# Where the split weights and their activations start within 128 bytes of SBUF

## The chip, the cores and the metric

The kernel runs on one core of one Trainium2 chip. TensorE multiplies, VectorE and ScalarE split operands and do the pointwise work, GpSimd (POOL) issues the gathers, SyncE (SP) issues the weight transfers. The metric is the device time of one launch in microseconds, the median of three runs.

## The reference

One token block of 256 tokens x 2048 channels goes through two layers in float32. Everything below is computed by this kernel in one launch (cut to what matters):

```python
def first_block(x, ...):                      # gated linear attention, then SwiGLU
    h = rms_norm(x, g0)
    x = x + gla_mixer(h, w_in, ...) @ w_out   # w_in: 2048 x 6144 (+16)
    x = x + (silu(g) * u) @ w_down            # g, u = split(rms_norm(x, g1) @ w_gu), 2 x 5632 wide

def hybrid_layer(h, mem, ...):
    proj = rmsnorm(h, norm_mix) @ w_in        # queries, keys, values of two attentions
    o_nsa = nsa_attention(...)                # compressed, selected and window branches
    o_sb = stick_breaking_attention(q_sb, k_sb, v_sb)
    h = h + concatenate([o_nsa, o_sb]) @ w_out
    h = h + memory_attention(rmsnorm(h, g), rmsnorm(mem, g2), w_q, w_k, w_v, w_o)
    h = h + peer_ffn(rmsnorm(h, g3), w_pq, sub_keys, u_tab, v_tab)
    return h                                  # then one last rmsnorm

def peer_ffn(hn, w_pq, sub_keys, u_tab, v_tab):
    # 8 heads x 16 experts of 16384 per token: a row of u_tab for the hidden value,
    # a row of v_tab for the output
    a = einsum('td,ted->te', x, u_tab[expert])
    return einsum('te,ted->td', gate * gelu(a), v_tab[expert])
```

## The kernel before

**Tiles.** All dense weights come as one stream of 292 tiles of 1 MB ([128 partitions, 2048 numbers], that is 512 rows by 512 columns of a weight matrix, 4 row blocks of 128 by 512 columns). SyncE brings them into a ring of four slots, `ring`. ScalarE rounds each half tile (a unit) to the short float format of TensorE's fast mode and writes it to `WH` (L487 to L490, with the norm's gain as scale in most stages); VectorE writes what rounding left, weight minus leading part, to `WL` (L502, L506). Each of `WH` and `WL` holds four units of 4096 bytes per partition, two tiles in all.

**Activations** are split in the same way into a leading and a remaining part, turned so that channels lie on the partitions: `HH` and `HL`, [128, 16, 256] each, for all normed inputs and for the output of the stick-breaking attention, and pairs in the arena for others: `Y_h`/`Y_l` (output of the linear attention), `A_h`/`A_l` (the SwiGLU hidden values), `N_h`/`N_l` (output of the first attention), `MN_h`/`MN_l` (normed memory) and `MO_h`/`MO_l` (output of the memory attention).

**The product.** `three` (L608 in the profile) issues three matmuls for each pair: leading x leading, leading x rest, rest x leading. `chunk` has two forms. In form T the weights are stationary (128 x 128) and the activations move (256 columns): 4 row blocks x 4 column blocks x 3 = 48 matmuls a tile. In form N the activations are stationary (128 tokens) and the weights move (512 columns): 4 row blocks x 2 token blocks x 3 = 24 matmuls a tile. In the profile's names the moving operand comes first: `ps<-WH,HH` is form N, `ps<-HH,WH` form T.

| stage | us in the trace | tiles, form | activations |
|---|---|---|---|
| linear attention, input | 12 to 345 | 16 T, 32 N | HH, HL |
| linear attention, output | 346 to 445 | 16 N | Y |
| gate and up | 445 to 935 | 88 N | HH, HL |
| down | 935 to 1185 | 44 N | A |
| second block, input | 1196 to 1508 | 32 T, 12 N | HH, HL |
| attentions' output | 1509 to 1618 | 8 N, 8 N | N; HH, HL |
| memory keys, values, query | 1618 to 1695 | 4 T, 4 N, 4 T | MN, MN; HH, HL |
| memory output | 1706 to 1729 | 4 N | MO |
| expert query | 1731 to 1830 | 16 T | HH, HL |

(The four tiles of the compression weights are used unsplit, at L916.) After that the expert stage gathers rows of `peer_u` and `peer_v` by token into twelve slots of `rows`, which lie over ring, WH, WL, HL and HH. VectorE takes dot products (L2449) and scaled sums (L2453) of them, TensorE takes the rest of the sums and 32 dense rows as products in full float32 (L1241, L1230, L1221).

**Order.** Nothing is scheduled by a tool: each engine's program is written out by hand with its waits, and the order of all instructions is that of the source.

**Places.** `place` puts a tensor at a byte address of the partition, one after the other; `take` cuts pieces from `arena`, and `split_views` makes the arena's pairs. All pieces of the arena that concern this change are multiples of 128 bytes long, so they start where the arena starts within 128 bytes:

```python
        rows, _ = place("rows", [P, ROWS, D])
        ring, at = place("ring", [P, RING, TILE], at=at)
        WH, at = place("WH", [P, UNITS, UNIT], f32r, at)
        WL, at = place("WL", [P, UNITS, UNIT], f32r, at)
        HL, at = place("HL", [P, KD, TOK], f32r, at)
        HH, at = place("HH", [P, KD, TOK], f32r, at)
```

## Time and profile before

| | us |
|---|---|
| median of 3 runs | 3087.81 |
| lowest and highest run | 3081.02, 3088.20 |
| span of the profiled execution, first to last instruction | 3083.2 |
| TensorE busy in it | 2723.6 |
| VectorE busy in it | 2111.9 |

A profiled execution is one run with the profiler on; its span leaves out what lies before the first and after the last instruction. Matmuls overlap: one is on record for 280 to 400 ns, from its first read to its last write, while the next one starts long before that. How fast TensorE goes is therefore read from the distance between two starts, in the view of instructions in order of time, and not from the duration of one. Some matmul records are missing from the trace, so counts are taken from the program.

### The profile page before, as it was taken

Reading aid. Unit: us, or ns where it says so; the run is one execution under the profiler, and the core shown is the slowest. Engines: PE = TensorE matmul, PEld = TensorE weight load, DVE = VectorE, ACT = ScalarE, POOL = GpSimd, SP = SyncE. Lnnn points to the kernel's source line nnn. Section 1 sums busy time; section 2 is a strip of 40 time slices with the busy share of each in tenths; the row PEclk is TensorE's granted clock in tenths of the full one; section 3 lists DMA queues with packets and bytes.
Section 4 is the critical chain, followed back from the end, with each engine's and each line's share of the span. In section 5 each row is a group of like instructions: output and inputs, shape, how many; then the busy total and the mean of one; then the engine's idle time right before and its main releaser. Section 6 shows DMA issues by size and latency. Waiting matters only on the chain.

```text
span 3083.2 us, 34652 instructions
## 1 busy us (share of the span) xinstructions
PE 2723.6 (88%) x12212; PEld 1969.0 (64%) x12212; DVE 2111.9 (68%) x2870; ACT 1146.2 (37%) x1980; POOL 988.0 (32%) x567
## 2 busy tenths in 40 slices
PE   9999999999999999999999975666666877669997
PEld 8888788888887888999889872222223433235433
DVE  5687665555564545445566688887888887679877
ACT  5455555555553335445665530000002330034000
POOL 0021000000000000000000038777778777878864
PEclk9999999999999999999999997898999888988999
DMA  7444455555555555453354459999999999999997
GB/s 271 151 155 164 173 178 183 189 190 190 190 177 191 184 185 183 178 182 135 127 191 173 164 228 415 419 409 410 408 417 411 416 407 402 420 376 383 409 402 305
DMA packets 123586, 827.89 MB, mean 269 GB/s; under 512 B 22167, under 2 KB 22183, under 8 KB 23855
## 3 DMA queue, kind: packets, MB, share of 16 engines
q0 software_dynamic: 79392, 510.36, 40.8%
q1 hardware_dynamic: 43920, 313.73, 28.5%
q10 hardware_dynamic: 144, 2.10, 0.2%
q8 instruction: 78, 1.28, 0.2%
q14 instruction: 52, 0.43, 0.0%
HBM read 892.00 MB, written 4.22 MB: 291 GB/s over the span
## 4 chain that ended last, share of the span: by engine, by line
PE 58%; POOL 14%; DMA 11%; DVE 9%; issue 5%; ACT 3%; DVEq 0%; SPq 0%; ACTq 0%
PE ps L608 49%; POOL rows L1324 14%; DMA rows<-peer_u,arena 7%; PE ps L1230 2%; DMA rows<-peer_v,arena 2%; DMA rows<-peer_v 2%; DVE arena L2449 2%; PE ps L1241 2%; DVE WL L506 1%; PE ps L716 1%; ACT arena L1800 1%; DVE arena L209 1%; DVE arena L202 1%; PE ps L916 0%; DVE arena L203 0%
## 5 line engine op out<-in xcount | busy, mean ns | idle before, releaser
L506 DVE SCALAR_TENSOR_TENSOR WL<-ring,PA,WH 128x512 fp32r<-128x512 f32 x896 | 633.1, 753 | 461.7 <-ACT WH L490 445.1
L1241 PE MATMUL ps<-rows,rstd 128*128 128x512 f32 x1164 | 629.6, 694 | 300.1 <-DMA rows<-peer_v,arena 216.9
L2449 DVE CUSTOM_DVE_ANT_0 arena<-rows,arena 128x2048 f32<-128x2048 f32 x256 | 586.9, 2293 | 155.7 <-DMA rows<-peer_u,arena 128.9
L1241 PEld LDWEIGHTS ps<-rows,rstd 128*128 128x128 f32 x1164 | 245.8, 221 | 670.5 <-issue 371.9
L1324 POOL DMA_INDIRECT rows<-peer_v,arena x256 | 484.0, 1891 | 196.8 <-DVE arena L2449 73.4
L489 ACT ACTIVATE WH<-ring,PA 128x512 fp32r<-128x512 f32 x448 | 324.2, 724 | 550.1 <-PE ps L608 401.7
L1324 POOL DMA_INDIRECT rows<-peer_u,arena x256 | 451.4, 1763 | 165.7 <-DVE WL L506 85.9
L608 PE MATMUL ps<-WH,HH 128*128 128x512 f32 x1120 | 442.8, 395 | 4.0 <-DVE WL L506 4.0
L608 PE MATMUL ps<-WH,HL 128*128 128x512 f32 x1120 | 438.0, 391 | 0.0
L608 PE MATMUL ps<-WL,HH 128*128 128x512 f32 x1120 | 437.9, 391 | 0.0
L490 ACT ACTIVATE WH<-ring,PA 128x512 fp32r<-128x512 f32 x448 | 317.2, 708 | 0.0
L608 PE MATMUL ps<-HH,WH 128*128 128x256 f32 x1088 | 310.2, 285 | 6.3 <-DVE WL L506 4.7
L608 PE MATMUL ps<-HH,WL 128*128 128x256 f32 x1088 | 308.6, 284 | 0.0
L608 PE MATMUL ps<-HL,WH 128*128 128x256 f32 x1088 | 308.5, 284 | 0.0
L2453 DVE SCALAR_TENSOR_TENSOR XR<-rows,arena,XR 128x2048 f32<-128x2048 f32 (+1 forms) x112 | 260.2, 2324 | 52.4 <-DMA rows<-peer_v,arena 42.6
L1297 POOL DMA_DIRECT2D arena<-bias_rows x2 | 1.8, 908 | 905.5 <-DVE XR L2157 905.5
L502 DVE TENSOR_TENSOR WL<-ring,WH 128x1024 fp32r<-128x1024 f32 x128 | 155.9, 1224 | 166.0 <-ACT WH L487 165.4
L1789 ACT ACTIVATE rstd<-CO,arena 128x128 f32<-128x128 f32 x147 | 53.6, 396 | 551.2 <-PE ps L1241 533.9
L608 PEld LDWEIGHTS ps<-WH,HH 128*128 128x128 f32 x1120 | 211.4, 189 | 49.2 <-DVE WL L506 5.4
L608 PEld LDWEIGHTS ps<-WH,HL 128*128 128x128 f32 x1120 | 211.4, 189 | 44.6
L608 PEld LDWEIGHTS ps<-WL,HH 128*128 128x128 f32 x1120 | 211.5, 189 | 43.2 <-issue 0.5
L1230 PE MATMUL ps<-rows,arena 128*128 128x512 f32 x512 | 223.8, 597 | 10.1 <-DMA rows<-peer_v 10.0
(367 smaller groups left out, 3538.0 us busy)
## 6 DMA issues: line engine op xcount, KB each, us to landing
ring<-stream SPq DMA_DIRECT2D x292, 1024.0 KB, 4.8
rows<-peer_v POOLq DMA_DIRECT2D x32, 1024.0 KB, 15.4
rows<-peer_u,arena POOLq DMA_INDIRECT x256, 14.8
rows<-peer_v,arena POOLq DMA_INDIRECT x256, 15.0
arena<-xT SPq DMA_DIRECT2D x4, 512.0 KB, 9.3
bias_rows<-bias_scratch POOLq DMA_DIRECT2D x1, 2048.0 KB, 10.5
arena<-xT ACTq DMA_DIRECT2D x1, 2048.0 KB, 9.5
arena<-memT POOLq DMA_DIRECT2D x1, 2048.0 KB, 10.7
```

The costliest lines, as they stand in the source:

```text
L202: ch.post(V.max_index(i[:, 0:8], v[:, 0:8], s))
L489: nc.scalar.activation(half_tile(WH, u)[:, 0:CH], raw_half(u)[:, 0:CH], ACT.Copy, scale=gain[0])
L490: nc.scalar.activation(half_tile(WH, u)[:, CH:UNIT], raw_half(u)[:, CH:UNIT], ACT.Copy, scale=gain[1]).then_inc(hi_done, 1)
L502: nc.vector.tensor_tensor(half_tile(WL, u), raw_half(u), half_tile(WH, u).bitcast(f32), ALU.subtract).then_inc(split, 1)
L506: ins = nc.vector.scalar_tensor_tensor(out=half_tile(WL, u)[:, s], in0=raw_half(u)[:, s], scalar=gain[d], in1=half_tile(WH, u).bitcast(f32 ...
L608: last = mm(o, l, r, start=start and n == 0, stop=stop and n == 2)
L1230: last = mm(ps[:, 4 * tt + q, :], DENSE_H[tt][:, c, :], rows[:, SLOTS[n % ROWS], q * CH:(q + 1) * CH], start=tt == 0 and c == 0, stop=tt = ...
L1241: last = mm(ps[:, 4 * tt + q, :], DIAG[:, k % DIAGS, :], rows[:, SLOTS[n % ROWS], q * CH:(q + 1) * CH], start=n == mine[0], stop=n == ends[q])
L1324: nc.gpsimd.indirect_dma_start(out=rows[:, SLOTS[n % ROWS], :], out_offset=None, in_=u_tab if tab == "u" else v_tab, in_offset=bass.Indire ...
L1789: A(DIAG[:, k % DIAGS, :], ident, ACT.Copy, scale=GA[:, g // PEER_H, at:at + 1]).then_inc(sem("diagonals"), 1)
L2449: ins = V.tensor_tensor_reduce(out=JUNK, in0=rows[:, SLOTS[n % ROWS], :], in1=HN[:, tt, :], scale=1.0, scalar=0.0, op0=ALU.mult, op1=ALU.a ...
L2453: ins = V.scalar_tensor_tensor(out=XN[:, tt, s], in0=rows[:, SLOTS[n % ROWS], s], scalar=GA[:, tt, at:at + 1], in1=XN[:, tt, s], op0=ALU.m ...
```

## The change

It changes addresses and nothing else: every engine's list of instructions, waits and DMAs is the same row by row; only the tensors that they name have other places.

| bytes past a multiple of 128 | before | after |
|---|---|---|
| WH, WL | 0 | 32 |
| HH, HL, linear attention input | 0 | 32 |
| HH, HL, gate and up (norm1) | 0 | 0 |
| HH, HL, second block input (norm2) | 0 | 64 |
| HH, HL, stick-breaking output (sb) | 0 | 0 |
| HH, HL, memory query and expert query (norm3, norm4) | 0 | 64 |
| arena, and Y, A, N, MO in it | 32 | 0 |
| MN | 32 | 32 |
| slots of ring and rows | 0 | 0, 64 by turns |
| rstd | 32 | 32 |
| XR | 0 | 0 |

HH and HL become six pairs of views, one for each use, over the same space (`H_AT`). The slots of `ring` and `rows` grow from 8192 to 8256 bytes (`SLOT`), so that the space of two slots holds WH, WL, HL or HH with up to 128 bytes to spare (`PAIR`). What that takes from the arena is won back: `GE` and `DGM` move to the place of small weights whose time does not overlap theirs, `CA` and `EQ` of the expert choice to `rstd`.

```diff
+SLOT = TILE + 16
+PAIR = 2 * 4 * SLOT
+W_SHIFT = 32
...
-        rows, _ = place("rows", [P, ROWS, D])
-        ring, at = place("ring", [P, RING, TILE], at=at)
-
-
-        WH, at = place("WH", [P, UNITS, UNIT], f32r, at)
-        WL, at = place("WL", [P, UNITS, UNIT], f32r, at)
-        HL, at = place("HL", [P, KD, TOK], f32r, at)
-        HH, at = place("HH", [P, KD, TOK], f32r, at)
-        XR, at = place("XR", [P, TT, D], at=at)
+        rows_all, end = place("rows", [P, ROWS, SLOT])
+        rows = rows_all[:, :, 0:D]
+        ring_all, at = place("ring", [P, RING, SLOT], at=at)
+        ring = ring_all[:, :, 0:TILE]
+
+
+        WH, _ = place("WH", [P, UNITS, UNIT], f32r, at + W_SHIFT)
+        WL, _ = place("WL", [P, UNITS, UNIT], f32r, at + PAIR + W_SHIFT)
+        H_AT = {}
+        for name, shift in (("gla", 32), ("norm1", 0), ("norm2", 64), ("sb", 0), ("norm3", 64), ("norm4", 64)):
+            low, _ = place("HL_" + name, [P, KD, TOK], f32r, at + 2 * PAIR + shift)
+            lead, _ = place("HH_" + name, [P, KD, TOK], f32r, at + 3 * PAIR + shift)
+            H_AT[name] = lead, low
+        XR, at = place("XR", [P, TT, D], at=end)
+        GE, _ = place("GE", [P, 4, 4 * N_CMP], at=at)
+        DGM, _ = place("DGM", [P, TT, P], at=at + 1024)
...
+        at += -at % 128
         N_ARENA = (SB_END - at) // 4
...
-        MNH, MNL, c = split_views("MN", b, KD)
+        MNH, MNL, c = split_views("MN", b + 8, KD)
...
-        CA, _ = take(a, 256)
-        EQ, a = take(a, 2, 16, 16)
+        CA = rstd[:, 0, :]
+        EQ = rstd[:, 0:2, :].rearrange("p a (b c) -> p a b c", c=16)
...
-                chunk(c + n, T_GU + 4 * n, XX, "N", i=i, i_pair=i, part=(0, 1))
+                chunk(c + n, T_GU + 4 * n, H_AT["norm1"], "N", i=i, i_pair=i, part=(0, 1))
```

## Rows read from the trace of the kernel before

**Rows 1.** The page, span and busy time of each engine (us, share, instructions).

```profile
span 3083.2 us, 34652 instructions
...
PE 2723.6 (88%) x12212; PEld 1969.0 (64%) x12212; DVE 2111.9 (68%) x2870; ACT 1146.2 (37%) x1980; POOL 988.0 (32%) x567
```

**Rows 2.** The page, the chain that ended last, by engine and by line.

```profile
PE 58%; POOL 14%; DMA 11%; DVE 9%; issue 5%; ACT 3%; DVEq 0%; SPq 0%; ACTq 0%
PE ps L608 49%; POOL rows L1324 14%; DMA rows<-peer_u,arena 7%; PE ps L1230 2%; DMA rows<-peer_v,arena 2%; DMA rows<-peer_v 2%; DVE arena L2449 2%; PE ps L1241 2%; DVE WL L506 1%; PE ps L716 1%; ACT arena L1800 1%; DVE arena L209 1%; DVE arena L202 1%; PE ps L916 0%; DVE arena L203 0%
```

**Rows 3.** Busy time by stretch: us, each engine, PEclk, DMA share, GB/s.

```profile
core 0: us, PE busy (x) PEld busy (x) DVE busy (x) ACT busy (x) POOL busy (x), PEclk, DMA share, GB/s
445.00:935.00 490.00, 490.00 (x2207) 405.61 (x2206) 287.50 (x430) 263.34 (x422) 0.00 (x0) 1.00 0.54 189
935.00:1185.00 250.00, 248.10 (x1058) 199.30 (x1057) 126.91 (x117) 98.06 (x103) 0.00 (x0) 0.99 0.51 183
...
1830.00:2300.00 470.00, 294.47 (x589) 117.89 (x588) 390.05 (x637) 36.09 (x108) 362.98 (x203) 0.87 1.01 413
2300.00:2800.00 500.00, 368.02 (x1030) 180.44 (x1028) 404.40 (x553) 132.86 (x355) 396.17 (x215) 0.87 0.99 403
2800.00:3083.00 283.00, 257.56 (x628) 114.95 (x628) 227.03 (x108) 17.67 (x38) 188.25 (x122) 0.97 0.93 377
```

**Rows 4.** Groups of L608: count, busy us, mean ns, idle us before, releaser.

```profile
L608 PE MATMUL ps<-WH,HH 128*128 128x512 f32 x1120 | 442.8, 395 | 4.0 <-DVE WL L506 4.0
...
L608 PE MATMUL ps<-HH,WH 128*128 128x256 f32 x1088 | 310.2, 285 | 6.3 <-DVE WL L506 4.7 <-issue 1.7
...
L608 PE MATMUL ps<-WH,A_h 128*128 128x512 f32 x352 | 140.0, 398 | 0.8 <-ACT arena L1487 0.8
```

**Rows 5.** In order of time (start us, us): gate and up, form N, HH and HL.

```profile
599.75 0.39 PE L608 MATMUL ps<-WH,HH 128*128 128x512 f32 x1
...
606.10 0.39 PE L608 MATMUL ps<-WL,HH 128*128 128x512 f32 x1
```

**Rows 6.** In order of time: down, form N, A in the arena.

```profile
999.75 0.40 PE L608 MATMUL ps<-WH,A_l 128*128 128x512 f32 x1
...
1006.99 0.40 PE L608 MATMUL ps<-WH,A_h 128*128 128x512 f32 x1
```

**Rows 7.** In order of time: memory values, form N, MN in the arena.

```profile
1649.61 0.40 PE L608 MATMUL ps<-WL,MN_h 128*128 128x512 f32 x1
...
1653.81 0.40 PE L608 MATMUL ps<-WL,MN_h 128*128 128x512 f32 x1
```

**Rows 8.** In order of time: second block input, form T, HH and HL.

```profile
1219.72 0.28 PE L608 MATMUL ps<-HH,WL 128*128 128x256 f32 x1
...
1223.44 0.28 PE L608 MATMUL ps<-HH,WH 128*128 128x256 f32 x1
```

**Rows 9.** In order of time: memory keys, form T, MN in the arena.

```profile
1621.73 0.28 PE L608 MATMUL ps<-MN_h,WH 128*128 128x256 f32 x1
...
1625.00 0.28 PE L608 MATMUL ps<-MN_l,WH 128*128 128x256 f32 x1
```

**Rows 10.** In order of time: rank projection, 16 stationary columns.

```profile
109.06 0.28 PE L608 MATMUL ps<-HH,AGH 128*16 128x256 f32 x1
...
113.03 0.28 PE L608 MATMUL ps<-HH,AGL 128*16 128x256 f32 x1
```

**Rows 11.** Groups by line and shape, all stages, columns as in rows 4.

```profile
L506 DVE SCALAR_TENSOR_TENSOR WL<-ring,PA,WH 128x512 fp32r<-128x512 f32 x896 | 633.1, 753 | 461.7 <-ACT WH L490 445.1 <-DVE arena L2115 9.9 <-DVE arena L1975 1.6
L1241 PE MATMUL ps<-rows,rstd 128*128 128x512 f32 x1164 | 629.6, 694 | 300.1 <-DMA rows<-peer_v,arena 216.9 <-ACT rstd L1789 82.9
L2449 DVE CUSTOM_DVE_ANT_0 arena<-rows,arena 128x2048 f32<-128x2048 f32 x256 | 586.9, 2293 | 155.7 <-DMA rows<-peer_u,arena 128.9 <-DVE arena L2428 3.6 <-DVE arena L2480 2.8
...
L2453 DVE SCALAR_TENSOR_TENSOR XR<-rows,arena,XR 128x2048 f32<-128x2048 f32 x109 | 256.4, 2352 | 52.2 <-DMA rows<-peer_v,arena 42.6 <-DVE arena L2506 2.1 <-DVE XR L2488 0.2
...
L1230 PE MATMUL ps<-rows,arena 128*128 128x512 f32 x512 | 223.8, 597 | 10.1 <-DMA rows<-peer_v 10.0
```

More of the change, by code:

```diff
@@ L333, in hybrid_block @@
         VC, a = take(a, 2, P, parts=N_CMP)
-        GE, a = take(a, 4, 4 * N_CMP)
         PC = PA[:, W_GATE:W_GATE + TT * NSA_H * N_CMP].rearrange("p (a b c) -> p a b c", b=NSA_H, c=N_CMP)
@@ L350, in hybrid_block @@
         MS, a = take(a, 64)
-        DGM, a = take(a, TT, P)
         PQ, a = take(0, KD, TOK)
@@ L654, in turn @@
                 last.then_inc(sem("turned"), 1)
-            XX = (HH, HL)
             pe.wait_ge(sem("gains_in"), 16)
@@ L666, in _ @@
                 if j == 4:
-                    chunk(1, T_GLA_IN + 4, XX, "T", part=(0, 1))
+                    chunk(1, T_GLA_IN + 4, H_AT["gla"], "T", part=(0, 1))
                 if j >= 4:
@@ L672, in _ @@
                 last.then_inc(sem("raw_turned"), 1)
-            chunk(1, T_GLA_IN + 4, XX, "T", part=(1, 4))
+            chunk(1, T_GLA_IN + 4, H_AT["gla"], "T", part=(1, 4))
             pe.wait_ge(sem("gla_inputs_in"), 32)
@@ L739, in _ @@
             for i in range(16):
-                chunk(4 + i // 2, T_GLA_IN + 16 + 4 * (i // 2), XX, "N", part=(2 * (i % 2), 2 * (i % 2) + 2))
+                chunk(4 + i // 2, T_GLA_IN + 16 + 4 * (i // 2), H_AT["gla"], "N", part=(2 * (i % 2), 2 * (i % 2) + 2))
                 if i in LEVEL_AFTER:
@@ L807, in chunk_raw @@
                     pe.wait_ge(sem("norm_split"), turn_count(name, 2 * q + 1))
-                    chunk(c, t, XX, form, part=(q, q + 1))
+                    chunk(c, t, H_AT[name], form, part=(q, q + 1))
             chunk(c + 2, T_GLA_OUT + 8, (YH, YL), "N", part=(0, 2))
@@ L900, in _ @@
             for k in range(4):
-                chunk(c, IN2_AT[0], XX, "T", ready=("norm_split", turn_count("norm2", (2, 2, 3, 4)[k])), part=(k, k + 1))
+                chunk(c, IN2_AT[0], H_AT["norm2"], "T", ready=("norm_split", turn_count("norm2", (2, 2, 3, 4)[k])), part=(k, k + 1))
             for n, form in list(enumerate("TTTTN"))[1:]:
-                chunk(c + n, IN2_AT[n], XX, form)
+                chunk(c + n, IN2_AT[n], H_AT["norm2"], form)
             pe.wait_ge(sem("small_weights"), 4)
+            HH, HL = H_AT["norm2"]
             for k in range(KD):
@@ L1047, in in2_part @@
                 n = 5 + i // 2
-                chunk(c + n, IN2_AT[n], XX, "T" if n < 9 else "N", part=(lo, hi))
+                chunk(c + n, IN2_AT[n], H_AT["norm2"], "T" if n < 9 else "N", part=(lo, hi))
             for i in range(11):
@@ L1111, in _ @@
                 if j == 4:
-                    chunk(c + 1, T_OUT2 + 4, XX, "N", part=(3, 4))
+                    chunk(c + 1, T_OUT2 + 4, H_AT["sb"], "N", part=(3, 4))
                 if j >= 4:
@@ L1119, in out2_chunk @@
                 chunk(c + n, T_OUT2 + 4 * n, NX, "N", part=(0, 2))
-                chunk(c + n, T_OUT2 + 4 * n, XX, "N", part=(2, 4))
+                chunk(c + n, T_OUT2 + 4 * n, H_AT["sb"], "N", part=(2, 4))
             out2_chunk(2)
@@ L1128, in _ @@
             chunk(c + 3, T_OUT2 + 12, NX, "N", part=(0, 2))
-            chunk(c + 3, T_OUT2 + 12, XX, "N", part=(2, 4))
+            chunk(c + 3, T_OUT2 + 12, H_AT["sb"], "N", part=(2, 4))
             c = chunk_of["mem"]
@@ L1139, in _ @@
             chunk(c + 1, T_MEM + 4, (MNH, MNL), "N", part=(0, 2))
-            chunk(c + 2, T_MEM + 6, XX, "T", ready=("norm_split", turn_count("norm3", 7) - 3))
+            chunk(c + 2, T_MEM + 6, H_AT["norm3"], "T", ready=("norm_split", turn_count("norm3", 7) - 3))
             chunk(c + 1, T_MEM + 8, (MNH, MNL), "N", part=(2, 2.5))
@@ L1190, in _ @@
                 else:
-                    chunk(c + n, T_PQ + 4 * n, XX, "T")
+                    chunk(c + n, T_PQ + 4 * n, H_AT["norm4"], "T")
                 if n == 0:
@@ L1360, in _ @@
                 act.wait_ge(sem(f"x_in{g}"), 16)
-                A(HH[:, 4 * g:4 * g + 4, :], XT[:, 4 * g:4 * g + 4, :], ACT.Copy).then_inc(sem("raw_leading"), 1)
+                A(H_AT["gla"][0][:, 4 * g:4 * g + 4, :], XT[:, 4 * g:4 * g + 4, :], ACT.Copy).then_inc(sem("raw_leading"), 1)
                 if g < 2:
@@ L1873, in rest_turned @@
                 s = (slice(None), slice(4 * q, 4 * q + 4), slice(tt * P, (tt + 1) * P))
-                rest(ps[:, bank, :].rearrange("p (k t) -> p k t", t=P), HH[s], HL[s], "norm_split")
+                rest(ps[:, bank, :].rearrange("p (k t) -> p k t", t=P), H_AT[name][0][s], H_AT[name][1][s], "norm_split")
             def add_chunk(c, t, n, per):
@@ L1907, in _ @@
                 s = slice(4 * g, 4 * g + 4)
-                rest(XT[:, s, :], HH[:, s, :], HL[:, s, :], "raw_split")
+                rest(XT[:, s, :], H_AT["gla"][0][:, s, :], H_AT["gla"][1][:, s, :], "raw_split")
                 if g < 2:
```

29 lines of the change are left out of this document (15 added, 14 removed).

## The prediction

> **What bounds the kernel now.** I read the page first, then the table by stage, then single starts of matmuls. TensorE is busy 88% of the span of 3083.2 us [rows 1], and the chain that ended last lies 49% on the matmuls of L608, the three products that each weight tile is used for [rows 2]. By stage there are two regimes [rows 3]. Up to about 1830 us TensorE is busy without a break (490.0 of 490 us in the gate-up stage, 248.1 of 250 in the down projection) while the DMA engines are half used and VectorE works 59% and 51% of the time. After that the expert rows arrive at 413 and 403 GB/s with a DMA share of 1.01 and 0.99, and TensorE is busy 63% and 74%. The big groups of L608 waited next to nothing: 4.0 us before all the WH,HH matmuls, 6.3 before the HH,WH ones, 0.8 before the WH,A_h ones [rows 4]. So in the first regime time is the number of matmuls times the distance between two starts; nothing else has to be costed there, and nothing is hidden behind something longer.
>
> That distance is not what the columns alone need. The granted clock is 1.00 and 0.99 of 2.4 GHz in these two stages [rows 3], so 512 columns are 213.3 ns and 256 are 106.7 ns. The rows show:
> - form N (512 moving weight columns), turned activations in HH and HL: 28 steps from 599.75 to 606.10, 226.8 ns each, 13.5 over its columns [rows 5];
> - form N, activations in the arena: 31 steps from 999.75 to 1006.99, 233.5 ns, 20.2 over [rows 6]; the memory stage's form N, MN_h and MN_l, 18 steps from 1649.61 to 1653.81, 233.3 ns, the same [rows 7];
> - form T (weights stationary, 256 moving activation columns) with HH and HL: 31 steps, 3.72 us, 120.0 ns, 13.3 over [rows 8];
> - form T with MN_h and MN_l, in the arena: 28 steps, 3.27 us, 116.8 ns, 10.1 over [rows 9].
>
> All four run the same instruction on tiles of the same shape. What differs is where the operands start within 128 bytes: weights 0, HH and HL 0, arena 32. Write d for the start of the moving operand less that of the stationary one. d = 0 costs 13.3 to 13.5 ns over the columns in both forms; d = +32 (form T, arena) costs 10.1; d = -32 (form N, arena) costs 20.2. That the extra is alike for 256 and 512 columns at d = 0 says that it is a price per matmul, as if the next stationary tile, loaded meanwhile, took reads from the moving stream. The MN tiles carry the argument: the same buffers are dear as stationary operand and cheap as moving one, so it isn't the arena that is slow but the pairing.
>
> The Trainium skill (SBUF — State Buffer, Who interferes with whom) says the contrary: TensorE has two independent read ports, one for the moving operand and one for the weight load, and "PE and ACT never wait on anyone". By it these addresses cost nothing and the change gives 0; the trace disagrees, with 226.8 against 233.5 ns.
>
> **The change part by part.** No instruction is added, removed or moved. WH and WL go to 32, the arena to 0, HH and HL to 32 (first stage), 0 (gate-up, stick-breaking output), or 64 (norm2, norm3, norm4). The law "the extra depends on d alone, in both forms" gives 223.4 ns for form N at d = +32 (213.3 + 10.1), an estimate from [rows 5, 9]. Matmuls are counted from the tiles: 24 a tile in form N, 48 in form T.
> - Gate-up, 88 tiles, and the stick-breaking half of the output projection, 8: d from 0 to +32, 2304 matmuls x (226.8 - 223.4) = 7.8 us saved.
> - Form N with activations in the arena: A 44 tiles, Y 16, N 8, MO 4, together 1728 matmuls, d from -32 to +32: x (233.5 - 223.4) = 17.5 us saved.
> - Form T with HH and HL at 64: projection of the second block 32 tiles, memory query 4, expert query 16: 52 x 48 = 2496 matmuls, d from 0 to +32, x (120.0 - 116.8) = 8.0 us saved.
> - Form N of the second block's projection, 12 tiles, 288 matmuls: weights 32 as moving, activations 64 as stationary, d from 0 to -32: x 6.7 = 1.9 us lost.
> - MN, moved with the weights so that d becomes 0: 96 matmuls of form N save 0.6 us, 192 of form T lose 0.6: nothing.
> - First stage, 48 tiles, 1536 matmuls: both at 32, d stays 0: nothing.
>
> Sum: 7.8 + 17.5 + 8.0 - 1.9 = 31.4 us. A little of it meets the few waits for splits, norms and the memory attention, 1.9 us in the down projection's 250 [rows 3]; I take 30.
>
> The bounds of the two sizes that no row shows. Form N at d = +32 lies between 213.3 (nothing over the columns) and 233.5 (the dear value); I take 223.4 because the two forms agree at d = 0. Form T at 64 against 32 has d = +32 with both starts shifted; it lies between the columns' 106.7 and the 126.8 that form N's dear extra would make, and I take the MN row's value. The nearest row to a weight load that costs little is the rank projection in the first stage, with 16 stationary columns: 35 steps from 109.06 to 113.03, 113.4 ns, still 6.7 over [rows 10]. I take that as the practical floor.
>
> The rest moves too, at nothing. The ring's and the rows' slots lie 8256 bytes apart, every second one 64 past a multiple of 128. ScalarE and VectorE, which read them in the first regime, have slack: one L506 takes 753 ns [rows 11], four a tile make 3.0 us against 24 x 0.2268 = 5.4 us of matmuls. Without that cover it would take VectorE 1.8 times as slow. In the expert stage a dot takes 2293 ns and a scaled add 2352 [rows 11], and VectorE is busy 390 of 470 us [rows 3]; it would become the bound there only if these grew by a fifth. The dot reads rows at 0 and the arena at 32, the add rows and XR at 0, and nothing in the rows says that either would care. TensorE's 512-column products of full float32 take 694 and 597 ns and wait for rows, 300.1 us before L1241 [rows 11]; they stream slower than the split products and I price them at 0. The stage's own bound, the DMA share, I expect unchanged: no row shows a packet to a slot 64 off, so its price is between a small gain and a loss, and I take 0. GE, DGM, CA and EQ are small tiles that get other places at no other order or wait.
>
> The sum is made against one profiled execution with a span of 3083.2 us; the three runs gave 3081.0 to 3088.2 us, median 3087.8, so span and runs agree within 5 us and I take the saving off the median: 3087.8 - 30 = 3058 us.
>
> **The rivals.**
> 1. The load is hidden better than by the law at +32, down to the floor of [rows 10]: 6.7 over the columns everywhere where d = +32. Then 2304 x 6.8 = 15.7, 1728 x 13.5 = 23.3, 2496 x 6.6 = 16.5, less 1.9: 53.6 us, 3034 us. For it: the extra falls with d at every step seen. Against: the one row at +32 shows 10.1, not 6.7. The Trainium skill (TensorE: Matmul & The Clock Gate, Back-to-back issue gap) gives 215.8 and 109.2 ns for isolated matmuls; at these the sum would be about 80 us, an estimate from that page, and no steady row of L608 comes near it.
> 2. It is not d but each operand's own place: a stationary tile at 32 costs 6.7 ns more, a moving one at 32 saves 3.2 to 3.4. The rows of before can't exclude it, since the weights only ever stood at 0. Now the weights stand at 32. First stage 1536 x 3.4 = 5.2 lost, form T at 64 2496 x 6.7 = 16.7 lost, MN in form T 1.3 lost; gate-up and its like 7.8, arena 17.5 and the rest 1.3 saved: 3.4 us faster, 3084 us, no change that can be told. Against it: an operand that costs when it is stationary and saves when it is moving is odder than a distance.
> 3. Addresses do nothing to TensorE (the ports' independence), and the 6.7 ns have another cause, for instance that arena tiles are being written nearby: 3088 us. MN in its two forms speaks against it.
> 4. Slower: in form N the distance counts without its sign, so that any 32 bytes between the streams costs 20.2 ns. Then gate-up and its like lose 2304 x 6.7 = 15.4 us, the arena stages stay, the second block's form N loses 1.9 and form T still saves 8.0: 9.3 us more, 3097 us. It decides at one number: as soon as form N at +32 is above 227 ns, gate-up turns from gain to loss, and as soon as it is above about 229 to 230 the whole gain is small. For it: form N at +32 has no row. Against: form T at +32 is cheaper, not dearer, with the same extra at 0.
> 5. The expert stage loses: packets to the slots 64 off take 1% longer on half of the rows, about 6 us of its 1253 us, which eats a fifth of the gain.
>
> **How the numbers follow.** The forecast, 3050 to 3065 us, has 0.56; rival 1 0.13, rival 2 0.14, rival 3 0.04, rival 4 0.09, and 0.04 for a loss as in rival 5 that is larger than the gain. A measurement of this kernel tells about 0.3% (9 us) from no change: faster is below 3078.5, slower above 3097.1. Faster takes the forecast, rival 1 and a little of rival 2: 0.72. Within 0.3% are rivals 2 and 3 and part of 4: 0.20. Slower 0.08. The range goes from rival 1, 3034, rounded to 3033, to rival 2 with 2 us for the spread, 3086; left out are rivals 3 and 4, the loss, and the part of rival 1 below the floor.
>
> **What would show it.** In the profile of the changed kernel: starts in the gate-up stage about 223.4 ns apart instead of 226.8, the stage some 7 us shorter; starts in the down projection 223.4 instead of 233.5, the stage 10.7 us shorter; form T with HH and HL at 64 at 116.8; first stage unchanged at 226.8 and 120.0; the second block's form N at 233.5; MN at 120.0 and 226.8. Rival 2 shows at once in the first stage (230 and 123 ns), rival 4 in gate-up (233.5), rival 1 in 220 ns. The stretch after 1830 us, about 1253 us, must keep its length. I would be wrong most of all if what I call d has another period or depends on the form, so that form N at +32 is anything but 223.4.

## The result and the profile after

The changed kernel takes 3092.4 us (median of 10 executions, 3089.4 to 3094.4) against 3083.6 us for the kernel before on the same chip (10 executions, 3076.1 to 3088.2). The ratio is 1.0031, 95% interval 1.0022 to 1.0039: 8.8 us slower, where the prediction had 3058 us and a gain. Measured once more on another chip the ratio was 1.0014 [1.0002, 1.0027]; where the second value differs from the first is told with that run.

The head of the page of the changed kernel, to be read against [rows 1]: the same 12212 matmuls, TensorE busy 12.8 us longer (2736.4 against 2723.6), the span 8.9 us longer.

```profile
span 3092.1 us, 34652 instructions
PE 2736.4 (88%) x12212; PEld 1964.7 (64%) x12212; DVE 2112.7 (68%) x2870; ACT 1146.7 (37%) x1980; POOL 986.1 (32%) x567
```

The table by stage, as [rows 3], over the linear attention's form N, gate and up, the down projection and the expert stage (columns: length, then busy us and count of TensorE, its weight loads, VectorE, ScalarE and GpSimd, granted clock, DMA share, GB/s):

```profile
119.00:345.00 226.00, 221.14 (x1075) 180.67 (x1075) 169.65 (x211) 124.85 (x175) 25.77 (x9) 0.99 0.42 151
446.00:947.00 501.00, 501.00 (x2199) 404.31 (x2198) 286.87 (x429) 263.14 (x421) 0.00 (x0) 1.00 0.51 183
948.00:1194.00 246.00, 244.08 (x1058) 197.85 (x1057) 126.51 (x117) 97.81 (x102) 0.00 (x0) 1.00 0.52 185
1841.00:3092.00 1251.00, 923.79 (x2238) 415.96 (x2236) 1020.87 (x1296) 186.04 (x500) 945.16 (x537) 0.89 0.98 401
```

In gate and up TensorE is still busy without a break and the granted clock is still 1.00: no wait and no clock has come in, the same matmuls simply stand further apart. Single starts say by how much. TensorE's timeline (start us, duration of one, engine, line, output and inputs) in gate and up, at the place of [rows 5]; 31 steps from the first to the last row:

```profile
599.64 0.40 PE L617 MATMUL ps<-WH,HL_norm 128*128 128x512 f32 x1
599.88 0.39 PE L617 MATMUL ps<-WH,HH_norm 128*128 128x512 f32 x1
600.11 0.39 PE L617 MATMUL ps<-WL,HH_norm 128*128 128x512 f32 x1
...
606.88 0.39 PE L617 MATMUL ps<-WH,HH_norm 128*128 128x512 f32 x1
```

7.24 us for 31 steps are 233.5 ns, where [rows 5] have 226.8 and the prediction wanted 223.4. The down projection, at the place of [rows 6], again 31 steps:

```profile
999.68 0.40 PE L617 MATMUL ps<-WH,A_l 128*128 128x512 f32 x1
...
1006.85 0.40 PE L617 MATMUL ps<-WH,A_h 128*128 128x512 f32 x1
```

231.3 ns against 233.5: a gain of 2, not of 10. Form T of the second block, at the place of [rows 8], and its form N, where the prediction had its one loss:

```profile
1219.78 0.28 PE L617 MATMUL ps<-HH_norm,WL 128*128 128x256 f32 x1
...
1223.45 0.28 PE L617 MATMUL ps<-HH_norm,WH 128*128 128x256 f32 x1
```

```profile
1511.81 0.40 PE L617 MATMUL ps<-WL,HH_norm 128*128 128x512 f32 x1
...
1516.94 0.39 PE L617 MATMUL ps<-WH,HL_norm 128*128 128x512 f32 x1
```

31 steps of 118.4 ns (120.0 in [rows 8], 116.8 expected), and 22 steps of 233.2 ns, where 233.5 was expected. Stage lengths, each from its first start to the first start of the next, in two traces of each kernel ("again" is a second execution of the same program, told of further down; "expected" is the prediction's change):

| stage | before | again | after | again | expected change |
|---|---|---|---|---|---|
| linear attention, form T | 107.5 | 108.7 | 107.5 | 106.3 | 0 |
| linear attention, form N | 226.5 | 225.5 | 226.5 | 227.8 | 0 |
| its output, Y | 99.0 | 99.0 | 99.4 | 99.3 | -3.9 |
| gate and up | 490.0 | 490.0 | 502.8 | 502.9 | -7.2 |
| down | 250.5 | 249.0 | 246.8 | 246.6 | -10.7 |
| second block, input | 324.0 | 323.0 | 323.7 | 324.9 | -3.0 |
| attentions' output | 109.3 | 109.3 | 110.6 | 110.6 | -2.6 |
| memory and expert query | 211.5 | 212.0 | 211.2 | 211.0 | -4.1 |
| expert rows | 1253.1 | 1253.2 | 1251.8 | 1244.0 | 0 |

One stage makes the result: gate and up, 12.8 us longer.

### The profile page after: what moved, and what is told of

It reads as the page before. It is cut to its first block, busy times and chain, and to the rows that moved or that the text cites. A ratio compares the mean times of both kernels' runs of the same rounds, so it can differ in the third digit from the quotient of the medians.

```text
span 3092.1 us, 34652 instructions
## 1 busy us (share of the span) xinstructions
PE 2736.4 (88%) x12212; PEld 1964.7 (64%) x12212; DVE 2112.7 (68%) x2870; ACT 1146.7 (37%) x1980; POOL 986.1 (32%) x567
## 4 chain that ended last, share of the span: by engine, by line
PE 23%; POOL 13%; DVE 10%; DMA 8%; issue 4%; ACT 2%; DVEq 0%; ACTq 0%
PE ps L617 14%; POOL rows L1334 13%; DMA rows<-peer_u,arena 6%; PE ps L1240 5%; DVE arena L2459 3%; DMA rows<-peer_v 1%; PE ps L1251 1%; ACT arena L1810 1%; DMA rows<-peer_v,arena 1%; DVE WL L515 1%; DVE arena L212 1%; DVE arena L205 1%; DVE arena L206 0%; PE ps L1231 0%; DVE arena L209 0%
## 5 line engine op out<-in xcount | busy, mean ns | idle before, releaser
L1334 POOL DMA_INDIRECT rows<-peer_v,arena x256 | 477.8, 1866 | 196.4 <-issue 65.5
L498 ACT ACTIVATE WH<-ring,PA 128x512 fp32r<-128x512 f32 x448 | 324.0, 723 | 560.4 <-PE ps L617 412.2
L617 PE MATMUL ps<-WH,HL_norm 128*128 128x512 f32 x800 | 318.6, 398 | 0.0
L617 PE MATMUL ps<-WH,HH_norm 128*128 128x512 f32 x800 | 318.0, 398 | 0.0
L617 PE MATMUL ps<-WL,HH_norm 128*128 128x512 f32 x800 | 314.6, 393 | 0.0
L617 PE MATMUL ps<-HH_norm,WH 128*128 128x256 f32 x832 | 236.4, 284 | 5.6 <-DVE WL L515 3.9
L617 PE MATMUL ps<-HL_norm,WH 128*128 128x256 f32 x832 | 234.2, 282 | 0.0
L617 PE MATMUL ps<-HH_norm,WL 128*128 128x256 f32 x832 | 234.2, 282 | 0.0
L496 ACT ACTIVATE WH<-ring 128x1024 fp32r<-128x1024 f32 x128 | 134.7, 1059 | 175.2 <-PE ps L617 167.8
L1240 PEld LDWEIGHTS ps<-rows,arena 128*128 128x128 f32 x512 | 97.9, 192 | 135.2 <-issue 118.8
L617 PEld LDWEIGHTS ps<-WL,HH_norm 128*128 128x128 f32 x800 | 150.8, 189 | 36.9
## 6 DMA issues: line engine op xcount, KB each, us to landing
bias_rows<-bias_scratch POOLq DMA_DIRECT2D x1, 2048.0 KB, 10.7
arena<-memT POOLq DMA_DIRECT2D x1, 2048.0 KB, 10.7
```

Of the source, the lines that this page charges most:

```text
L496: nc.scalar.activation(half_tile(WH, u), raw_half(u), ACT.Copy).then_inc(hi_done, 1)
L498: nc.scalar.activation(half_tile(WH, u)[:, 0:CH], raw_half(u)[:, 0:CH], ACT.Copy, scale=gain[0])
L617: last = mm(o, l, r, start=start and n == 0, stop=stop and n == 2)
L1240: last = mm(ps[:, 4 * tt + q, :], DENSE_H[tt][:, c, :], rows[:, SLOTS[n % ROWS], q * CH:(q + 1) * CH], start=tt == 0 and c == 0, stop=tt = ...
L1334: nc.gpsimd.indirect_dma_start(out=rows[:, SLOTS[n % ROWS], :], out_offset=None, in_=u_tab if tab == "u" else v_tab, in_offset=bass.Indire ...
```

## The experiments

What all of them ask is the same: how far apart do matmuls start, as a function of where their two operands lie. m is the start of the moving operand, s that of the stationary one, in bytes. A "three" is what `three` issues for one pair: leading x leading, leading x rest, rest x leading. Where a spacing is given for a whole stage, it is the mean over the stage's steps without a wait.

### m1_scan: the disputed cost by itself

A kernel that is not the block: it fills one buffer, and TensorE alone then works off bursts of 16 equal matmuls at chosen offsets, with a 64-column matmul as a mark between bursts. No other engine works meanwhile and no DMA runs. Some bursts take their offsets in threes as the kernel does.

```
matmul(ps[:, bank, 0:n], BIG[:, s:s + 128], BIG[:, m:m + n], start=True, stop=True)   # n = 512 or 256
```

> Not the block: only bursts of matmuls of the short float format from one large buffer, with nothing else running. After a warm-up, each burst is 16 matmuls with one moving and one stationary operand, behind a small 64-column matmul as a mark; the first burst has both operands at 0 past a multiple of 16384, then the moving one goes up in steps of 16 bytes to 496, then the stationary one, then both together, then form T in steps of 32. At the end the triples of the kernel are replayed with the places of before and of after. The theory of one distance with a sign (d, moving less stationary): 226.8 ns at d = 0, 233.5 at the stationary operand 32 further, about 223 at the moving one 32 further, the same along every line of equal d. Rival, distance without a sign in form N: 233 at both. Rival, not the operands at all but the writes of ScalarE and VectorE near them: the same spacing in every burst. Rival, distances over 128 matter, since WL now lies 16512 past WH and not 16384: the curve over 512 bytes does not repeat after 128, and the replayed triples of after differ from the same triples without the extra 128.

Measured, ns between starts: form N 227 at m = s = 0, 233.3 at m = 32, 232.9 at s = 32; form T 120 at 0, 116.9 at m = 32, 118.2 at s = 32. The threes with the kernel's own offsets gave 226.9 for HH and HL before (kernel 226.8), 233.1 for A before (233.5), 229.2 for the linear attention after (229.3), 233.5 for gate and up after (233.5) and 231.0 for A after (231.3; this burst has the arena 128 bytes from its place in the kernel modulo 256). So TensorE's own reads are enough to give these spacings: the buffers' neighbours, ScalarE, VectorE and the DMAs are not needed for them. In form N the sign of the 32 bytes doesn't matter, and adding 512 to 16384 bytes to the moving operand of such a burst changes nothing, while 128 does.

Two things in the same scan limit this. At odd multiples of 16 bytes the distance does not decide: m = s = 16 or 48 settles at 233.3 ns, as dear as 32 apart, and m = 0 with s = 16 at 226.7, as cheap as equal places. No operand of the kernel lies at such a place; what follows holds for multiples of 32. And the threes of Y after took 233.5 ns against 231.0 for those of A, though the two bursts differ only in the place of the remaining part, by 8192 bytes. In the kernel it is 234.5 for Y and 231.3 for A.

The Trainium skill (SBUF — State Buffer, Who interferes with whom) gives TensorE independent read ports for the two operands; with nothing but TensorE at work the bursts still differ, 227 against 233, so the measurement speaks against that independence as far as the places are concerned.

### e1_gateup_at_0, e2_all_at_0, e3_T_plus_32: parts of the change undone

The first gives gate and up the weights' own 32 bytes. (The label says 0: it is the distance to the weights that is 0.)

```diff
-        for name, shift in (("gla", 32), ("norm1", 0), ("norm2", 64), ...
+        for name, shift in (("gla", 32), ("norm1", 32), ("norm2", 64), ...
```

> The changed kernel with one number different: HH and HL of the gate-up stage at 32 and not at 0, so that weights and activations are again at one phase there, as in the first stage. The sum by stages gave gate-up 12.8 us more than before and all else 4 less. If the distance of 32 is what costs there, gate-up comes back by 2112 x (233.2 - 229.3) = 8 us at the spacing that the first stage shows in form N, and the kernel is about 3084, level with before. If the place of the weights alone costs (32 instead of 0), gate-up keeps 233 ns and the kernel stays at 3092.

3082.6 us, ratio 0.9996 [0.9985, 1.0007]: the loss is gone. Gate and up takes 494.5 us instead of 502.8. The timeline of TensorE there, 28 steps:

```profile
599.73 0.39 PE L617 MATMUL ps<-WL,HH_norm 128*128 128x512 f32 x1
...
606.13 0.39 PE L617 MATMUL ps<-WH,HL_norm 128*128 128x512 f32 x1
```

228.6 ns, where the kernel before has 226.8 at what was thought the same distance of 0. A remainder of 4.5 us stays in this stage; the 8.3 us that came back are the 8 expected.

> The changed kernel with every shift at 0: weights, all six pairs of activations, arena and MN start at multiples of 128. What is left of the change is the slots 8256 bytes apart and so WL 16512 past WH. If phase within 128 bytes is all, form N takes 226.8 ns everywhere, in the down projection and the other arena stages 6.5 less than before: 1824 x 6.5 = 12 us faster than before, 3072, and the expert stage is unchanged. If the extra 128 between WH and WL, HL and HH costs (the first stage at equal phase shows 229.3 after against 227.1 before), form N takes 229 and the kernel is near 3078. If the slots 64 off cost, the stretch after the expert query grows beyond 1253 us.

```diff
-W_SHIFT = 32
+W_SHIFT = 0
...
-        for name, shift in (("gla", 32), ("norm1", 0), ("norm2", 64), ...
+        for name, shift in (("gla", 0), ("norm1", 0), ("norm2", 0), ...
...
-        MNH, MNL, c = split_views("MN", b + 8, KD)
+        MNH, MNL, c = split_views("MN", b + 0, KD)
```

3068.7 us, ratio 0.9954 [0.9938, 0.9971]: with the arena at 0 and nothing shifted, what is left of the change is 0.5% faster. The down projection takes 244.4 us, yet gate and up 494.3, and form N stands at 229.0 everywhere, form T at 117.8 to 118.3. The time is better than either value expected (3072 and 3078): form N came at the dearer 229, but form T was 2 ns cheaper than the kernel before's 120, which neither value counted, and the expert stage took 1243.5 us in this trace instead of 1253. Form T in this kernel, at the place of [rows 8]; 33 steps of 117.9 ns, not 120.0, though every operand lies at 0 modulo 128:

```profile
1219.76 0.28 PE L617 MATMUL ps<-HL_norm,WH 128*128 128x256 f32 x1
...
1223.65 0.28 PE L617 MATMUL ps<-HL_norm,WH 128*128 128x256 f32 x1
```

Both forms leave [rows 5, 8] with all places alike modulo 128. What this kernel still has of the change, as far as these operands go, is the slots 8256 bytes apart: they put WL 16512 bytes behind WH, and HH as far behind HL, which is 128 modulo 256.

> As the run with every shift at 0, but HH and HL at 32 in the stages of form T with them (norm2, norm3, norm4) and MN at 32: form T at a distance of +32. Theory of the distance, T cheaper at +32 (116.8 to 118.5 measured, against 120.0): 2688 x 2 = 5 us faster than the run with every shift at 0, less 288 matmuls of form N that get a distance of -32 (1.9 us). Rival, T at +32 is cheap only where W stands as before or the buffers as before: no difference between the two runs.

```diff
-W_SHIFT = 32
+W_SHIFT = 0
...
-        for name, shift in (("gla", 32), ("norm1", 0), ("norm2", 64), ("sb", 0), ("norm3", 64), ("norm4", 64)):
+        for name, shift in (("gla", 0), ("norm1", 0), ("norm2", 32), ("sb", 0), ("norm3", 32), ("norm4", 32)):
```

3071.7 us, 0.9972 [0.996, 0.9983]. Form T with HH and HL 32 past the weights stands at 118.5 to 118.6, against 117.8 to 117.9 in e2; the second block's form N and MN's go to 233.3. Its median is 3 us above that of e2; the two intervals overlap, but in the traces the second block's input is 4.1 us longer (325.3 against 321.2). The 5 us expected from the shift by 32 for form T did not come: it is worth nothing at these slots.

### m2_fine: the period, and a finer scan

The same kernel as m1 with bursts of 32, m and s over a whole 256 bytes, some of them in steps of 8 and 16.

> Not the block: bursts of 32 matmuls again, each behind one small mark, now with form T in finer steps and with the kernel's triples in both forms. The first scan repeated after 256 bytes and not after 128, so every place here is given as the moving operand's start m and the stationary operand's start s modulo 256. Theory from it: form N is cheapest at m = s (226.9 in the triple) and pays 6 at 32 on either side; form T is cheapest at m - s = 64, near 113.5, against 120 at 0 and 117 to 118 at 32, and so in the triple of the kernel too. Rival: the 113.5 holds only for one operand pair repeated, and the triple of form T at 64 shows 117 or more, since HH's and HL's loads cross. The bursts that change one operand by turns tell whether a matmul's distance goes with its own stationary tile or with the next one's.

Bursts on TensorE's timeline (start, us of the burst of 32 matmuls; the first step of each is about 90 ns longer). Form N at m = 0, 32, 64, 96, 128 and 256, s = 0:

```profile
52.89 7.53 PE L111 MATMUL ps<-BIG 128*128 128x512 f32 x32
60.28 7.71 PE L111 MATMUL ps<-BIG 128*128 128x512 f32 x32
67.86 7.58 PE L111 MATMUL ps<-BIG 128*128 128x512 f32 x32
75.31 7.71 PE L111 MATMUL ps<-BIG 128*128 128x512 f32 x32
82.88 7.71 PE L111 MATMUL ps<-BIG 128*128 128x512 f32 x32
113.22 7.51 PE L111 MATMUL ps<-BIG 128*128 128x512 f32 x32
```

128 is as dear as 32, and 256 is as cheap as 0. Form T at m = 0, 32, 64, 192 and 256:

```profile
180.93 4.08 PE L111 MATMUL ps<-BIG 128*128 128x256 f32 x32
184.88 3.99 PE L111 MATMUL ps<-BIG 128*128 128x256 f32 x32
196.57 4.02 PE L111 MATMUL ps<-BIG 128*128 128x256 f32 x32
224.03 3.90 PE L111 MATMUL ps<-BIG 128*128 128x256 f32 x32
235.62 4.07 PE L111 MATMUL ps<-BIG 128*128 128x256 f32 x32
```

In ns between starts, with one operand at 0:

| m or s | 0 | 32 | 64 | 96 | 128 | 160 | 192 | 224 |
|---|---|---|---|---|---|---|---|---|
| N, m | 227.0 | 233.3 | 229.1 | 233.3 | 233.3 | 234.3 | 233.5 | 232.9 |
| N, s | 227.0 | 232.9 | 233.3 | 233.9 | 232.4 | 233.4 | 229.3 | 233.3 |
| T, m | 119.9 | 116.9 | 117.8 | 119.9 | 119.8 | 117.3 | 114.1 | 118.6 |
| T, s | 119.9 | 118.2 | 113.9 | 117.3 | 120.0 | 119.6 | 117.9 | 116.8 |

m = 256 and 320 repeat 0 and 64 (227.0, 229.2; 119.6, 117.8). With m = s at multiples of 32 form N settles at 226.7 (in m1) and form T at 119.7. So at multiples of 32 it is nearly the distance that counts (N at m = 64 equals N at s = 192, T at m = 192 about T at s = 64), but modulo 256 and by a table of its own for each form: form N is cheap at distance 0 alone, form T is dear there. The spacing of a three is not the mean of its parts, though: for A after the change the table gives (234.3 + 233.3 + 234.3) / 3 = 234.0, the kernel has 231.3, and for the burst of m1 and m2, at distances of 32, 160 and 32, it gives 233.6 where 231.0 was measured. Nor do the places modulo 256 settle it: there Y, N and MO lie where A does, and stand at 234.5, 235.3 and 235.6. MO shows that the same program can do both. Its rows in the first and in the second trace of the changed kernel:

```profile
1719.63 0.40 PE L617 MATMUL ps<-WH,MO_l 128*128 128x512 f32 x1
...
1722.46 0.40 PE L617 MATMUL ps<-WH,MO_l 128*128 128x512 f32 x1
```

```profile
1719.67 0.40 PE L617 MATMUL ps<-WH,MO_l 128*128 128x512 f32 x1
...
1722.45 0.40 PE L617 MATMUL ps<-WH,MO_l 128*128 128x512 f32 x1
```

12 steps of 235.8 and of 231.7 ns, with every address the same. Which operand's read meets which is open.

Written modulo 256 the changed kernel has WH at 160, WL at 32, HL and HH of gate and up at 128 and 0. All three of its products are then at distances of 160, 32 and 32, none of them cheap. In the kernel before, all four are at one phase, and only the arena is 32 off.

### x0_one_phase and x1_T_at_64: the slots brought to one phase modulo 256

```diff
+        WH, _ = place("WH", [P, UNITS, UNIT], f32r, at + 128)
+        WL, _ = place("WL", [P, UNITS, UNIT], f32r, at + PAIR)
...
+            low, _ = place("HL_" + name, [P, KD, TOK], f32r, at + 2 * PAIR + 128 - shift)
-        at += -at % 128
+        at += -at % 256
```

All shifts are 0 and MN starts at b + 0 (not shown), so weights, HH, HL and arena share one phase.

> As the run with every shift at 0, but WH, WL, HH, HL and the arena's pairs at one phase within 256 bytes and not within 128: WH 128 bytes further, HL too, so that WL is 16384 past WH and HL 16512 - 128 before HH. If the period is 256, form N goes from 229.1 back to 226.9 (5184 matmuls, 11 us less) and form T from 118.2 to 120.0 (3456 matmuls, 6 us more): about 5 us faster than the run with every shift at 0, 3064. Rival, the period is 128 and the 229.1 came from the larger slots: no difference, 3069.

3063.7 us where 3064 was expected, 0.995 [0.9936, 0.9963]; repeated on another chip (x0_again) 3064.1 us, 0.9943 [0.9928, 0.9958]. Gate and up is back at 490.0 us, exactly as before the change, the down projection takes 242.1, form N stands at 227 to 228 everywhere and form T at 119.9 to 120.0. This settles the 128 bytes, by the starts and stages (the intervals of the two times overlap): against e2 only WH and HL have moved, by 128 bytes, and form N gains the 2 ns that e2 lacked (488 us of gate and up now hold 2195 matmuls, there 2180). The first row is of e2, the second of x0_again (the same columns as in the table by stage):

```profile
446.00:934.00 488.00, 488.00 (x2180) 400.18 (x2179) 283.84 (x426) 261.31 (x417) 0.00 (x0) 1.00 0.51 187
446.00:934.00 488.00, 487.71 (x2195) 403.34 (x2194) 286.66 (x429) 263.25 (x420) 0.00 (x0) 1.00 0.53 189
```

x1 has, on top, HH at +64 and HL at -64 in the stages of form T:

> As the run at one phase, but where form T works on HH and HL (second block, memory query, expert query) HH starts 64 bytes past the weights' phase and HL 64 before it. By the bursts form T takes 113.4 at +64 and 114.0 at -64 against 120.0: 2496 x 6 = 15 us saved, 288 matmuls of form N in the second block pay 6.3 ns, 2 us: 13 us faster than the run at one phase, about 3051, 33 us or 1.1% faster than before. Rival, the triple mixes the two distances and gets 117 to 118: 2496 x 2.5 = 6 us, 3060.

3066.2 us, 0.9953 [0.994, 0.9967]: neither the 3051 us nor the rival's 3060, and the interval overlaps that of x0. In its trace form T stands at 117.0 to 117.6 instead of 120 and the second block is 2.2 to 3.3 us shorter than in x0's two traces, a gain too small for the times to show. The form N of that block pays 232 for it.

### m3: why 64 past gave two values

m1 had 113.4 ns at m = 64 in form T, m2 117.8 for the same matmul.

> Not the block: bursts of 40 matmuls with the same pair of operands, each behind a mark and one matmul of another number of columns (none, 64, 72, 96, 128, 200, 256, 384). In the first scan form T with m 64 past s took 113.4 ns and in the second 117.8, in bursts that differ only in what ran ahead. Theory: the two reads can lock in more than one way, and what ran ahead decides, so the same burst shows both values here. Rival: it was the PSUM bank or something else that is the same in each run, and then every burst of one pair shows one value, except perhaps those by bank. Form T at 192 (64 before s) and form N at 0 are expected at one value each, 114.0 and 227.

Bursts of 40 at m = 64, each behind one matmul of another width, which is the row ahead of it; TensorE's timeline:

```profile
82.99 0.36 PE L91 MATMUL ps<-BIG 128*128 128x256 f32 x1
83.19 4.87 PE L83 MATMUL ps<-BIG 128*128 128x256 f32 x40
...
87.93 0.42 PE L91 MATMUL ps<-BIG 128*128 128x384 f32 x1
88.19 4.70 PE L83 MATMUL ps<-BIG 128*128 128x256 f32 x40
```

Behind 256 columns a step takes 117.8 ns, behind 384 it takes 113.3, and it stays so through all 40. m = 192, for which one value was expected, is the other way round: 113.3 to 113.8 behind 64 to 256 columns, 117.8 behind 384. Behind the 64-column mark alone it took 117.8 too, where m2 had 114.0 behind the same mark, so more than the last matmul ahead plays a part:

```profile
92.72 0.19 PE L89 MATMUL ps<-BIG 128*128 128x64 f32 x1
92.75 4.96 PE L83 MATMUL ps<-BIG 128*128 128x256 f32 x40
```

m = 32 (116.7) and form N at 0 and 64 (227, 229.1) have one value each here, and for m = 64 the PSUM bank makes no difference (117.7 to 117.9). So form T at a distance of 64 on either side can lock into one of two rhythms, and the work ahead of it decides. What in the chip keeps the rhythm no run here shows.

### x2_T_64_before: a version that beats both

The kernel's own threes at -64 gave 113.8 ns in m2, at +64 117.8. x2 is x0 with HH and HL at -64 in the stages that begin in form T, and MN too; norm4's HH stays at +64.

```diff
+        for name, back, lead_at in (("gla", 64, -64), ("norm1", 0, 0), ("norm2", 64, -64), ("sb", 0, 0),
+                                    ("norm3", 64, -64), ("norm4", 64, 64)):
+            low, _ = place("HL_" + name, [P, KD, TOK], f32r, at + 2 * PAIR + 128 - back)
+            lead, _ = place("HH_" + name, [P, KD, TOK], f32r, at + 3 * PAIR + lead_at)
-            MNH, MNL, c = split_views("MN", b + 0, KD)
+            MNH, MNL, c = split_views("MN", b + 48, KD)
```

> The kernel at one phase within 256 bytes, but HH, HL in the first stage, the second block's input and the memory query, and MN, start 64 bytes before the weights' phase; for the expert query HL 64 before and HH 64 after it, since there the rows' slots leave no other place. By the bursts form T takes 114 ns at 64 before (120 at 0; 117.8 with the two mixed) and form N then 229.1 (226.9 at 0). Form T: 768 + 1536 + 192 + 192 matmuls x 6.2 = 16.7 us, expert query 768 x 2 = 1.5 us saved; form N: 768 + 288 + 96 matmuls x 2.2 = 2.5 us lost. Against the run at one phase 15.7 us faster: about 3048 to 3050, 1.0 to 1.1% under before. Rival, in the kernel the locked pattern of the bursts does not hold, because the matmuls wait for splits and other work at each half tile: form T takes 117 to 118 and the kernel is level with the run at one phase or 5 us faster.

> The kernel at one phase once more, on the same chip as the run above, to compare the two. It should give again 0.995 of before.

3056.0 us (3051.1 to 3058.2), ratio 0.9912 [0.9898, 0.9927], beside x0_again on the same chip at 0.9943: 26 us under the kernel before on the same chip, and 36 under the changed one's median on another. Form T of the second block in x0 and then in x2, at the place of [rows 8]:

```profile
1219.72 0.28 PE L616 MATMUL ps<-HH_norm,WH 128*128 128x256 f32 x1
...
1223.33 0.28 PE L616 MATMUL ps<-HH_norm,WH 128*128 128x256 f32 x1
```

```profile
1219.78 0.28 PE L616 MATMUL ps<-HL_norm,WH 128*128 128x256 f32 x1
...
1223.86 0.28 PE L616 MATMUL ps<-HL_norm,WH 128*128 128x256 f32 x1
```

30 steps of 120.3 ns, and 36 steps of 113.3. The block's input takes 316.5 us instead of 325.1, the first form T 103.7 instead of 107.1. Form N with the HH and HL at -64 pays 229.1 instead of 227.0, which is less than form T wins. norm4, at +64, stands at 117.6.

It expected 3048 to 3050 us and got half of the 15.7 us. Up to the expert rows the trace is 12.3 us shorter than that of x0_again (1804.7 against 1817.0), but the expert stage took 1249.7 us against 1243.7. And -64 isn't cheap everywhere in this kernel: form T averages 114.8 ns in the first stage and 114.5 in the second block's input, since some stretches run at 117.8, and MN, at -64 too, runs at 117.8 throughout, here in 31 steps:

```profile
1600.83 0.28 PE L616 MATMUL ps<-MN_l,WH 128*128 128x256 f32 x1
...
1604.48 0.28 PE L616 MATMUL ps<-MN_h,WL 128*128 128x256 f32 x1
```

Those are the two values of m3, now both inside one kernel.

### before_again and after_again: the expert stage

> The kernel before, unedited, profiled once more, for one question: the stage of the expert rows took 1253.1 us in its one trace and 1243 to 1250 us in the traces of the edited kernels, though no law of the operands' places speaks of it. Theory 1 (it differs from one execution to the next, whatever the places): a second trace gives a length somewhere between 1243 and 1254, not bound to 1253, and the same edit can give lengths 5 us apart. Theory 2 (the places of the kernel before cost the stage about 9 us, by the arena at 32 past or by the slots): again 1252 to 1254. Both expect all stages before it to keep their lengths within 1 us, but the first, whose start is not steady: gate and up 490.0, down 250.5, second block 324, and a ratio of 1.000.

> The changed kernel, unedited, profiled once more behind the kernel before on the same chip. Expert stage: theory 1 (it differs from one execution to the next) 1243 to 1254 us, not bound to the first trace's 1251.8; theory 2 (set by the places) 1251 to 1253 again. In both the TensorE stages repeat: gate and up 502.8, down 246.8, second block 323.7 us, and the ratio to the kernel before lies at 1.0025 to 1.004.

The kernel before once more: 3082.5 us, 0.9988 [0.9975, 1.0002]; the changed kernel 3087.6 us (3086.5 to 3093.5), 1.0014 [1.0002, 1.0027]. The stage of the expert rows took 1253.2 us in the second trace of before and 1244.0 in that of after, which had 1251.8 in the first. The two traces of the changed kernel in the same stretch, first and second (columns as in the table by stage):

```profile
1845.00:3055.00 1210.00, 896.51 (x2163) 403.68 (x2163) 990.99 (x1273) 177.49 (x487) 936.62 (x534) 0.89 1.00 408
1845.00:3055.00 1210.00, 890.20 (x2183) 400.69 (x2182) 997.05 (x1278) 177.85 (x487) 945.96 (x536) 0.90 1.00 410
```

One and the same program takes 8 us more or less for this stage, by the execution (408 and 410 GB/s in this stretch); what differed between the two executions these views don't show. The first trace is of an execution of 3093.9 us, the second of one of 3086.5, and the stages ahead of it agree within 0.5 us in sum (1840.3 and 1840.7). So a difference in this stage is enough for that between the two ratios, 1.0031 and 1.0014, whose intervals overlap anyway. For the changed kernel theory 1 (it differs from one execution to the next) holds. For the kernel before, twice at 1253, two traces can't exclude that its places cost the stage something: its total against x0 is about 18 us in the times, of which the stages of TensorE explain about 12 (1830.1 and 1827.7 us up to the expert rows, against 1817.4 and 1817.0). The other traces have 1248.0 (e1), 1249.7 (x2) and 1243.3 to 1244.2 us (e2, e3, x1 and both of x0). The rest stays open.

## Why the prediction was wrong

**What bounds the kernel** was right: up to the expert rows the time is the number of matmuls times the distance of two starts. The 2112 matmuls of gate and up times 233.2 - 227.0 ns are 13.1 us; the stage grew by 12.8.

**The step that failed** is the law, "the extra depends on d alone, in both forms". Three things in it were wrong.
- It carried form T's price at +32 into form N. That the forms agree at d = 0 was one coincidence and no law: in form N the scan has 233 at +32 and -32, in form T 116.9 and 118.2 to 118.6. So gate and up with its like did not gain 7.8 us; gate and up alone lost 12.8 (2112 x 6.2 = 13.1).
- The period is 256, not 128. The diff moved slots by 8256 bytes, and the prediction priced that for ScalarE, VectorE and the DMAs, but not for TensorE, whose WH and WL it put 128 apart modulo 256. By e2 against x0 this costs form N 2 ns. It also explains the first stage: its form N went to 229.3 and its form T to 117.8, both expected unchanged, which cancelled to within 1 us.
- With both, the arena's term failed: 17.5 us expected, 2 to 4 found in the down projection (231.3 against 233.3 ns, times 1056), and a small loss in Y, N and MO (234.5, 235.3, 235.6 against 233.2).

**Form T at 64** was expected at 116.8 and came at 118.6 to 118.9: 1.1 to 1.4 ns instead of 3.2, so 3 to 4 us of the 8.0. This is the period again. HH and HL were to lie 32 past the weights; modulo 256 two of the three products do, and HH with WH lies at 160 (64 less 160). The burst of m2 with these places took 118.6 ns, and e3, with the same three distances, 118.5 to 118.6, while the burst with all three at 32 took 116.7.

**The loss in the second block's form N** was right, 233.3 ns against 233.5, since -32 and +32 cost the same. **MN** was expected to change hands at no cost: 118.4 and 228.9 instead of 120.0 and 226.8, again the 128. **The expert stage**, ScalarE and VectorE were right in size: the stage did not grow, and the two are busy 1146.7 and 2112.7 us, against 1146.2 and 2111.9.

**The rivals.** Rival 4 was the right one, a distance that counts without its sign: 3097 us, +9.3, against a measured +8.8 and +4.1. That the totals are so close is in part luck: up to the expert rows the changed kernel is 10 and 13 us longer in the traces, form T saved 3 to 4 us of the 8.0 that the rival counted on, and the expert stage was 1 and 9 us shorter. It had 0.09, since "form T at +32 is cheaper, not dearer" was taken to speak of form N. That argument was worth little, as no row of form N stood at +32, and the whole gain of 25 us hung on that one unseen number. Its deciding point, 227 ns, was the right thing to watch. Rival 1's floor of 220 ns at +32 is excluded for form N: nothing in the scan is under 226.6. The isolated figures of 215.8 and 109.2 ns from the Trainium skill (TensorE: Matmul & The Clock Gate, Back-to-back issue gap) were not reached by any burst either, not even with TensorE alone; the lowest were 226.6 and 113.3. Rival 2, each operand's own place, falls with m = s: both at 32, 64 or 96 cost what both at 0 do. (At 16 and 48 both together do cost more, but there is no such place in the kernel.) Rival 3 falls with m1.

The last sentence of the prediction, that it would be wrong most of all if d "has another period or depends on the form", names both errors; the chance given to them was too small.

## What to carry over

In a stage that TensorE bounds, the starts of the two operands are worth 3% of every 512-column matmul and 6% of every 256-column one: bring weights, split activations and scratch to one phase modulo 256, at a multiple of 32, where the weights move in 512 columns, and look for the cheap distance (here -64) where activations move in 256. The second is less sure than the first: at -64 the same kernel ran at 113.3 or at 117.8 ns. Take a price at an offset only from a row with that offset, that form and that period; a law drawn through rows at two offsets is a guess at a third, and a scan by itself costs one small kernel. The scan of one pair is not the last word on a three: replay the order of the kernel too. When slots move by a number of bytes, write every operand's place out modulo the period before and after, for each engine that reads it.

## What the runs showed of the hardware

- The distance of back-to-back matmuls with a new weight tile each depends on the two operands' starts: 226.6 to 234.3 ns in 512 columns, 113.3 to 120.3 in 256, at a granted clock of 1.00 of 2.4 GHz, at multiples of 32 bytes and for one pair repeated. There it repeats after 256 bytes (m1), and it needs no other engine. At odd multiples of 16 equal places can cost 233.3 ns.
- In 256 columns a distance of 64 has two stable rhythms, 113.3 and 117.8 ns, chosen by the work ahead (m3), and both occur within x2. In 512 columns the threes of MO took 235.8 and 231.7 ns in two executions of one program.
- At multiples of 32 equal phase is the best case in 512 columns (226.7 ns) and nearly the worst in 256 (120.0).
- The expert stage of one program took 1251.8 and 1244.0 us in two executions, with nothing else changed.
